# The one-pass matmul helper with its columns in backward order

## The chip, the cores and the metric

The kernel runs on one NeuronCore of a Trainium2 chip. Its time is the device time of one execution in microseconds (us). The kernel before has a median of 864.19 us over three runs (864.02 to 864.34).

## The reference

Two stacked blocks act on 256 rows of width 1024, everything in fp32, batch 1, depth 1 and depth 2.

```python
def first_block(...):                       # 16 meta rows go ahead of x: 272 rows
    z = rms_norm(h_res) @ w_in              # 4 branch inputs, their gates, 4 x 1024 mixing gates
    m = sum(sigmoid(gl[b] + gate_bias[b]) * (branch_b(z) @ w_out_b) for b in pool, mla, conf, short conv)
    return (h_res + rms_norm(m @ w_o))[:, 16:]

def second_block(...):                      # layer 0: gated linear attention, layer 1: MoBA attention
    for i in range(2):
        y = gla_mixer(x) if i == 0 else moba_mixer(x)
        x = layer_norm(ALPHA * x + y)
        x = layer_norm(ALPHA * x + (silu(x @ w_gate) * (x @ w_up)) @ w_down)     # hidden width 2816
```

The work is mostly dense products with weights that are read once: `w_in`, the branch outputs, `w_o`, the attention projections, and two feed-forward layers.

## The kernel before, in words

Products must keep nearly fp32 accuracy, and the kernel gets it out of TensorE's one-pass format (fp32r). Each operand is held as two such parts: a high part, the value rounded by ScalarE (line 1272 for weights), and a low part, value minus high part, which VectorE computes (line 1709 for weights). A product is then three one-pass matmuls into the same PSUM columns: high x high, high x low, low x high. The helper `exact` (lines 595 to 599) issues these three. "Stationary" is the side that is loaded into the array as weights of a matmul, "moving" the side that streams through it column by column; PSUM columns are written in the order in which the moving columns come.

Weights come as 512 KB slots of 128 x 1024 values into a ring of nine (`staged`, with the parts `w_hi` and `w_lo`). SyncE's queue loads the slots in a fixed order; a slot is free for the next load when TensorE's semaphore `weights_used` says so. ScalarE and VectorE make the parts some slots ahead (`lead`). TensorE's program is one list written out by hand, stage after stage, and waits for semaphores only.

`exact` is called in these places:
- `t_slot` (lines 601 to 613): weights stationary, turned activations moving, 256 columns (x rows), 272 (with the meta rows) or 258 (the short convolution's rows, which begin two columns ahead of the 256, at column 14 of a 272-column row). It serves the input products and gates of the first block, and parts of the later ones.
- `y_slot` and `y_mla` (lines 885 and 982): the branch outputs, 256 columns.
- `n_slots` and `n_product` (lines 725 and 743): activations stationary, weights moving, 512 columns, for products whose result is wanted row by row.
- `down_half` (line 1133): the second feed-forward product, 512 columns; the very last quarter of the last layer is cut into two of 256, one of which goes to the bank `misc`.

Not through `exact` go: the first z product (`first_slots`, line 657), the wide stage of the feed-forward (`wide_slot`, lines 624 to 647, in which one matmul of 512 columns has the x high parts in its first 256 columns and the low parts in the others, followed or preceded by one of 256), the row-major first products (`n_first`, lines 688 to 723), the transposes, and the small products in full fp32.

`acc` is PSUM for the products, two pairs of two banks; a pair is written for one output while the other is read by ScalarE or VectorE. `misc` is four banks for everything small. A reader waits for the semaphore of the last matmul that writes its banks. The operands of `exact` are two-dimensional slices (partitions, columns) whose columns lie in one run.

Of the kernel before, what the change touches and what calls it, by code (L numbers as in the profile page):

```python
# [187 lines left out]
def lead_of(at):  # L188

    return min(LEAD, 3 + at // 2)  # L190


def hybrid_stack(nc, d, out):
    with ExitStack() as ctx:
# [389 lines left out]
        def _(pe):  # L584
# [9 lines left out]

            def exact(dst, st_hi, st_lo, mv_hi, mv_lo, start, stop):

                pe.matmul(dst, st_hi, mv_hi, start=start, stop=False)  # L597
                pe.matmul(dst, st_hi, mv_lo, start=False, stop=False)  # L598
                return pe.matmul(dst, st_lo, mv_hi, start=False, stop=stop)  # L599

            def t_slot(sl, p, half, mv_hi, mv_lo, kcs=4, last=True, halves=2, first=True):

                ready(sl)
                n = mv_hi.shape[-1]
                hi = w_hi[:, sl.ring(), :].rearrange("p (c n) -> p c n", c=4)
                lo = w_lo[:, sl.ring(), :].rearrange("p (c n) -> p c n", c=4)
                for b in range(halves):
                    for c in range(kcs):
                        cols = slice(b * P, b * P + P)
                        mm = exact(acc[:, p, b, 0:n], hi[:, c, cols], lo[:, c, cols],  # L610
                                   mv_hi[:, half * 4 + c, :], mv_lo[:, half * 4 + c, :],
                                   start=first and c == 0, stop=last and c == kcs - 1)
                mm.then_inc(weights_used, 1)
# [111 lines left out]
            def n_slots(stage, names, st_hi, st_lo, lo=0, hi=None):  # L725

                for i in range(lo, COUNT[stage] if hi is None else hi):
                    sl = Slot(FIRST[stage] + i, i)
                    q, name = i % 4, names[i // 4]
                    if q == 0:  # L730
                        open_out(name)
                    ready(sl)
                    for c in range(2):
                        cols = slice(c * 512, c * 512 + 512)
                        for t in range(TILES):
                            rows = slice(t * P, t * P + P)
                            k = q * 2 + c
                            mm = exact(acc[:, pair(name), t, :], st_hi[:, k, rows], st_lo[:, k, rows],
                                         w_hi[:, sl.ring(), cols], w_lo[:, sl.ring(), cols],
                                         start=k == 0, stop=k == KC - 1)  # L740
                    mm.then_inc(weights_used, 1)

            def n_product(stage, tag, st_hi, st_lo, chunks_ready):
# [3 lines left out]
                def quarter(i, t):  # L747

                    q, name = i % 4, names[i // 4]
                    sl = Slot(FIRST[stage] + i, i)  # L750
                    rows = slice(t * P, t * P + P)
                    if t == 0:
                        ready(sl)
                    for c in range(2):
                        cols = slice(c * 512, c * 512 + 512)
                        k = q * 2 + c
                        mm = exact(acc[:, pair(name), t, :], st_hi[:, k, rows], st_lo[:, k, rows],
                                   w_hi[:, sl.ring(), cols], w_lo[:, sl.ring(), cols], start=k == 0, stop=k == KC - 1)
                    if t == 1:
                        mm.then_inc(weights_used, 1)  # L760
                    elif q == 3:
                        mm.then_inc(s["tail_part"], 1)
# [311 lines left out]
            for j in range(4):  # L1074
                b = open_bank("o%d" % j)
                t = j // 2
                for i in range(2):
                    hd = j % 2 * 2 + i
                    dst = b[:, i * DV:(i + 1) * DV]
# [173 lines left out]
        def _(act):  # L1253
# [21 lines left out]
            def lead(sl):  # L1275
                round_slots(sl.at + lead_of(sl.at) + 1)
# [410 lines left out]
        def _(dve):  # L1687
# [24 lines left out]
            def lead(sl):  # L1712
                split_slots(sl.at + lead_of(sl.at) + 1)
# [877 lines left out]
```

## Time and profile before

| | |
|---|---|
| median of three runs | 864.19 us |
| the profiled execution's own time | 864.27 us |
| its span, first to last instruction | 862.5 us |
| PE (TensorE matmuls) busy | 850.2 us, 99% |
| PEld (weight loads, beside PE) busy | 757.6 us, 88% |
| DVE (VectorE) busy | 629.8 us, 73% |
| ACT (ScalarE) busy | 426.5 us, 49% |
| read from HBM | 151.48 MB, 177 GB/s over the span |

One execution is recorded by the profiler. Times within it are microseconds from the span's start. Matmuls are pipelined: the next one starts before the one before has ended, and a record's duration (281 ns for 256 columns) is longer than the step from one start to the next. That step is called the pitch below. PEclk is the TensorE clock that was granted, in tenths of full speed.

### The profile page before, as it was taken

The numbers are of one execution on the slowest core, as the hardware profiler recorded it, in microseconds if no ns is written. First come the engines' busy times: TensorE is split into PE (matmuls) and PEld (weight loads), VectorE is DVE, ScalarE is ACT, GpSimd is POOL, SyncE is SP. The second block draws the span as 40 slices with busy tenths as digits, with TensorE's granted clock in tenths as the row PEclk, the third lists the DMA queues.
The fourth block names the chain that finished last, engine by engine and source line by source line (L and its number), as shares of the span: only waits on it lengthen the run. The fifth ranks groups of instructions, "written<-read, shape, count | busy, mean of one in ns | idle before, by whom it ended". The sixth has DMA issues, their size and how long they took to land.

```text
span 862.5 us, 13049 instructions
## 1 busy us (share of the span) xinstructions
PE 850.2 (99%) x5390; PEld 757.6 (88%) x5390; DVE 629.8 (73%) x880; ACT 426.5 (49%) x613; POOL 79.3 (9%) x81
## 2 busy tenths in 40 slices
PE   8999999999999999999999999999999999999996
PEld 7998999999988987878888988889988888889885
DVE  5999857688586675796777764678987777777445
ACT  6646454456664874435444453256553544445320
POOL 0340100122003001011000000031100200000000
PEclk9999999999999999999999999999999999999998
DMA  9963776664356752557556555386544765665531
GB/s 289 270 188 92 203 203 174 181 184 123 100 169 192 238 171 86 171 169 245 184 184 193 195 186 192 117 278 195 178 142 129 244 189 183 191 195 184 187 118 50
DMA packets 121989, 154.46 MB, mean 179 GB/s; under 512 B 11663, under 2 KB 98090, under 8 KB 121930
## 3 DMA queue, kind: packets, MB, share of 16 engines
q1 hardware_dynamic: 119978, 148.23, 56.4%
q0 software_dynamic: 1872, 5.26, 1.8%
q8 instruction: 43, 0.70, 0.3%
q10 hardware_dynamic: 80, 0.13, 0.0%
q14 instruction: 16, 0.13, 0.0%
HBM read 151.48 MB, written 1.05 MB: 177 GB/s over the span
## 4 chain that ended last, share of the span: by engine, by line
PE 94%; DVE 4%; DMA 1%; issue 0%; ACT 0%; SPq 0%; DVEq 0%
PE acc L597 19%; PE acc L599 19%; PE acc L598 19%; PE acc L635 15%; PE acc L639 8%; PE acc L720 1%; PE acc L717 1%; PE acc L718 1%; PE acc L668 1%; PE misc L798 1%; DMA x<-in_x 1%; DVE x L2191 1%; PE misc L857 1%; DVE y L2172 1%; DMA staged<-in_moba_w_in 1%
## 5 line engine op out<-in xcount | busy, mean ns | idle before, releaser
L1709 DVE TENSOR_TENSOR w_lo<-staged,w_hi 128x1024 fp32r<-128x1024 f32 (+1 forms) x274 | 331.6, 1232 | 134.6 <-ACT w_hi L1272 134.0
L1272 ACT CAST w_hi<-staged 128x1024 fp32r<-128x1024 f32 (+1 forms) x274 | 278.0, 1044 | 90.5 <-DMA staged<-in_ffn_w_down 44.2
L597 PE MATMUL acc<-x_parts,w_hi 128*128 128x256 f32 (+2 forms) x712 | 203.4, 286 | 0.0
L598 PE MATMUL acc<-x_parts,w_hi 128*128 128x256 f32 (+2 forms) x712 | 200.6, 282 | 0.0
L599 PE MATMUL acc<-x_parts,w_lo 128*128 128x256 f32 (+2 forms) x712 | 200.5, 282 | 0.0
L635 PE MATMUL acc<-x_parts,w_hi 128*128 128x512 f32 x576 | 196.3, 393 | 0.0
L639 PE MATMUL acc<-x_parts,w_lo 128*128 128x256 f32 x576 | 149.1, 279 | 0.0
L597 PEld LDWEIGHTS acc<-x_parts,w_hi 128*128 128x128 f32 x712 | 134.4, 189 | 1.7 <-issue 1.0
L598 PEld LDWEIGHTS acc<-x_parts,w_hi 128*128 128x128 f32 x712 | 134.0, 188 | 0.7 <-issue 0.2
L599 PEld LDWEIGHTS acc<-x_parts,w_lo 128*128 128x128 f32 x712 | 134.5, 189 | 0.0
L635 PEld LDWEIGHTS acc<-x_parts,w_hi 128*128 128x128 f32 x576 | 103.3, 188 | 18.4 <-DVE gate_sum L2352 0.2
L639 PEld LDWEIGHTS acc<-x_parts,w_lo 128*128 128x128 f32 x576 | 108.3, 188 | 6.4
L597 PE MATMUL acc<-w_hi,h_hi 128*128 128x512 f32 (+1 forms) x176 | 66.3, 377 | 0.0
L598 PE MATMUL acc<-w_lo,h_hi 128*128 128x512 f32 (+1 forms) x176 | 66.3, 377 | 0.0
L599 PE MATMUL acc<-w_hi,h_lo 128*128 128x512 f32 (+1 forms) x176 | 66.1, 376 | 0.0
L1619 ACT CAST h_hi<-hidden 128x512 fp32r<-128x512 f32 x22 | 13.7, 621 | 70.5 <-DVE hidden L2378 65.0
L597 PEld LDWEIGHTS acc<-w_hi,h_hi 128*128 128x128 f32 x176 | 33.1, 188 | 6.1
L599 PEld LDWEIGHTS acc<-w_hi,h_lo 128*128 128x128 f32 x176 | 33.1, 188 | 6.2
L598 PEld LDWEIGHTS acc<-w_lo,h_hi 128*128 128x128 f32 x176 | 33.1, 188 | 5.9
L2516 POOL TENSOR_TENSOR x_parts<-y,x_parts 128x512 fp32r<-128x512 f32 x8 | 10.4, 1295 | 297.1 <-ACT y L1482 297.1
L1478 ACT CAST x_parts<-misc 128x512 fp32r<-128x512 f32 (+1 forms) x20 | 9.6, 503 | 46.4 <-PE misc L798 46.4
L1609 ACT ACTIVATE h_gate<-gate_sum 128x512 f32<-128x512 f32 x16 | 10.1, 632 | 41.8 <-DVE gate_sum L2352 41.8
(394 smaller groups left out, 1256.0 us busy)
## 6 DMA issues: line engine op xcount, KB each, us to landing
staged<-in_ffn_w_gu SPq DMA_DIRECT2D x88, 512.0 KB, 3.6
staged<-in_w_in SPq DMA_DIRECT2D x58, 512.0 KB, 3.8
staged<-in_ffn_w_down SPq DMA_DIRECT2D x44, 512.0 KB, 3.3
staged<-in_gla_w_in SPq DMA_DIRECT2D x24, 512.0 KB, 4.3
staged<-in_moba_w_in SPq DMA_DIRECT2D x24, 512.0 KB, 3.9
staged<-in_w_o SPq DMA_DIRECT2D x8, 512.0 KB, 3.9
staged<-in_gla_w_out SPq DMA_DIRECT2D x8, 512.0 KB, 3.8
staged<-in_moba_w_out SPq DMA_DIRECT2D x8, 512.0 KB, 3.8
```

The lines of the kernel that those rows point to most:

```text
L597: pe.matmul(dst, st_hi, mv_hi, start=start, stop=False)
L598: pe.matmul(dst, st_hi, mv_lo, start=False, stop=False)
L599: return pe.matmul(dst, st_lo, mv_hi, start=False, stop=stop)
L635: return pe.matmul(acc[:, p, b, :].rearrange("p (s n) -> p s n", s=2), hi[:, c, cols], x_parts[:, :, k, 0:ROWS], start=k == 0, stop=k == K ...
L639: return pe.matmul(acc[:, p, b, 0:ROWS], lo[:, c, cols], x_hi[:, k, 0:ROWS], start=False, stop=False)
L668: mm = pe.matmul(acc[:, pair("z0"), b, 0:KEYS], st[:, c, b * P:b * P + P], mv[:, k, :], start=k == 0 and st is hi and mv is x_hi, stop=k = ...
L1272: nc.scalar.copy(hi, raw).then_inc(rounded, 1)
L1478: nc.scalar.copy(x_hi[:, lo:lo + n, t * P:t * P + P], bank(name)[:, 0:n * P] .rearrange("p (c r) -> p c r", c=n)).then_inc(s["x_rounded"], 1)
L1609: nc.scalar.activation(h_gate[:], gate_sum[:], ACT.Silu).then_inc(s["h_gated"], 1)
L1619: nc.scalar.copy(halves(h_hi, b), hidden[:]).then_inc(s["h_rounded"], 1)
L1709: nc.vector.tensor_tensor(lo, raw, hi, ALU.subtract).then_inc(split, 1)
L2516: nc.gpsimd.tensor_tensor(x_lo[:, 4 * j:4 * j + 4, 0:P], y[:, 0, j * 512:j * 512 + 512] .rearrange("p (c r) -> p c r", c=4), x_hi[:, 4 * j ...
```

## The change

A new function, `backwards`, takes an access pattern and returns the same columns from the last to the first: it starts at the last column and has the step negated. `exact` passes the PSUM destination and the moving sides through it. The stationary sides stay as they were.

```diff
+def backwards(ap):
+    step, n = ap.ap[-1]
+    return bass.AP(ap.tensor, ap.offset + step * (n - 1), list(ap.ap[:-1]) + [[-step, n]])
...
             def exact(dst, st_hi, st_lo, mv_hi, mv_lo, start, stop):
 
+                dst, mv_hi, mv_lo = backwards(dst), backwards(mv_hi), backwards(mv_lo)
                 pe.matmul(dst, st_hi, mv_hi, start=start, stop=False)
                 pe.matmul(dst, st_hi, mv_lo, start=False, stop=False)
                 return pe.matmul(dst, st_lo, mv_hi, start=False, stop=stop)
```

Since both are turned, each product column still lands in the PSUM column that it had.

## Rows read from the trace of the kernel before

**Rows 1.** The page: PE's busy time, granted clock by slice, chain that ended last.

```profile
PE 850.2 (99%) x5390; PEld 757.6 (88%) x5390; DVE 629.8 (73%) x880; ACT 426.5 (49%) x613; POOL 79.3 (9%) x81
...
PEclk9999999999999999999999999999999999999998
...
PE 94%; DVE 4%; DMA 1%; issue 0%; ACT 0%; SPq 0%; DVEq 0%
PE acc L597 19%; PE acc L599 19%; PE acc L598 19%; PE acc L635 15%; PE acc L639 8%; PE acc L720 1%; PE acc L717 1%; PE acc L718 1%; PE acc L668 1%; PE misc L798 1%; DMA x<-in_x 1%; DVE x L2191 1%; PE misc L857 1%; DVE y L2172 1%; DMA staged
...
by line: PE acc L597 19.1%; PE acc L599 19.0%; PE acc L598 19.0%; PE acc L635 15.5%; PE acc L639 7.8%; PE acc L720 1.4%; PE acc L717 1.1%; PE acc L718 1.1%; PE acc L668 0.7%; PE misc L798 0.7%; DMA x<-in_x 0.7%; DVE x L2191 0.6%; PE misc L8
```

**Rows 2.** Waits of PE on other engines: us in total, times, longest.

```profile
PE misc L808 <- POOL w_gk L2450: 1.4, 1, 1.4
PE misc L798 <- DVE x L2191: 1.3, 3, 0.4
PE misc L790 <- DVE rs L1760: 0.6, 1, 0.6
```

**Rows 3.** The chain's end: start, us, what.

```profile
853.81 0.13 PE misc L599
853.97 0.43 DVE y L2218
...
858.63 0.75 DVE x L2191
```

**Rows 4.** Timeline of PE, 256 columns: start, us, instruction.

```profile
100.34 0.28 PE L599 MATMUL acc<-x_parts,w_lo 128*128 128x256 f32 x1
...
142.58 0.28 PE L599 MATMUL acc<-x_parts,w_lo 128*128 128x256 f32 x1
```

**Rows 5.** Timeline of PE, 512 columns, feed-forward of layer 0.

```profile
501.50 0.40 PE L597 MATMUL acc<-w_hi,h_hi 128*128 128x512 f32 x1
...
547.75 0.39 PE L597 MATMUL acc<-w_hi,h_hi 128*128 128x512 f32 x1
```

**Rows 6.** Groups by form on PE, count, busy us, mean ns; and L597 over the span.

```profile
L597 PE MATMUL acc<-x_parts,w_hi 128*128 128x256 f32 x632 | 180.2, 285 | 0.0
L597 PE MATMUL acc<-w_hi,h_hi 128*128 128x512 f32 x154 | 60.2, 391 | 0.0
L597 PE MATMUL acc<-w_hi,x_parts 128*128 128x512 f32 x64 | 26.2, 409 | 0.0
L597 PE MATMUL acc<-x_parts,w_hi 128*128 128x272 f32 x48 | 14.1, 293 | 0.0
L597 PE MATMUL acc<-w_hi,mo_hi 128*128 128x512 f32 x32 | 13.0, 405 | 0.0
L597 PE MATMUL acc<-u_mla_hi,w_hi 128*128 128x256 f32 x32 | 9.2, 287 | 0.0
L597 PE MATMUL acc<-x_parts,w_hi 128*128 128x258 f32 x32 | 9.1, 283 | 0.0
L597 PE MATMUL misc<-w_hi,h_hi 128*128 128x256 f32 x22 | 6.2, 283 | 0.0
L597 PE MATMUL acc<-w_hi,h_hi 128*128 128x256 f32 x22 | 6.1, 279 | 0.0
L597 PE MATMUL acc<-u_sc_hi,w_hi 128*128 128x256 f32 x16 | 4.7, 293 | 0.0
...
0.00:862.50 862.50, 363.41 (x1150) 216.91 (x1150) 1.00 0.59 179
```

**Rows 7.** Timeline of PE, 258 columns that begin at column 14.

```profile
46.87 0.28 PE L597 MATMUL acc<-x_parts,w_hi 128*128 128x258 f32 x1
...
58.23 0.28 PE L599 MATMUL acc<-x_parts,w_lo 128*128 128x258 f32 x1
```

**Rows 8.** Timeline of PE, end of the wide stage.

```profile
486.75 0.39 PE L635 MATMUL acc<-x_parts,w_hi 128*128 128x512 f32 x1
486.98 0.28 PE L639 MATMUL acc<-x_parts,w_lo 128*128 128x256 f32 x1
...
489.88 0.40 PE L635 MATMUL acc<-x_parts,w_hi 128*128 128x512 f32 x1
```

**Rows 9.** Groups by form on VectorE.

```profile
L1709 DVE TENSOR_TENSOR w_lo<-staged,w_hi 128x1024 fp32r<-128x1024 f32 x272 | 330.2, 1236 | 134.6 <-ACT w_hi L1272 134.0
L2352 DVE TENSOR_REDUCE up_sum<-acc 128x512 f32<-128x1024 f32 x20 | 24.4, 1218 | 0.0
```

**Rows 10.** Waits of VectorE and ScalarE: us in total, times, longest.

```profile
DVE w_lo L1709 <- ACT w_hi L1272: 134.0, 115, 3.2
...
ACT w_hi L1272 <- DMA staged<-in_ffn_w_down: 44.2, 26, 2.3
```

## The prediction

> **What bounds the kernel now.** I read the page first, then who waits on TensorE, then its instructions by form, then the starts of single matmuls. The page shows PE busy for 99% of the span, and the chain that ended last lies on PE for 94%; the three lines of the edited helper alone carry 19.1%, 19.0% and 19.0% of that chain, which is 57.1% of 862.5 us or some 492 us [rows 1]. The granted clock is full (2.4 GHz) in every slice but the last [rows 1]. PE waits for another engine only in its first microseconds, 1.4 us at the longest, and before transposes of freshly normalised rows [rows 2]. After PE's last matmul at 853.8 us there follow some 8.7 us of VectorE and store [rows 3]. So from the first weights to 853.8 us the time is the sum of the pitches of PE's matmuls, from one start to the next, and whatever changes a pitch changes the span by the same amount: there is no cover for a longer one.
>
> The pitch, and not the duration of one, is what to price, since a matmul's duration overlaps the next one. I take it from long stretches without a wait. Between the two starts at 100.34 and 142.58 us there are 357 matmuls of 256 columns: 42.24 us / 357 = 118.3 ns [rows 4]. Between 501.50 and 547.75 us there are 204 of 512 columns: 46.25 / 204 = 226.7 ns [rows 5]. At 2.4 GHz, 256 columns are 106.7 ns and 512 are 213.3 ns, so streaming a column per cycle fills the pitch but for 11.7 ns and 13.3 ns.
>
> **The change part by part.** How many instructions it touches: the first of the three matmuls is issued 1150 times [rows 6], so 3450 of the 5390 matmuls [rows 1] are turned round. By form, the first line has 632 + 22 + 22 matmuls of 256 columns with x or hidden parts, 32 + 3 x 16 of 256 with branch rows, 48 of 272, 32 of 258, and 154 + 64 + 3 x 32 of 512 (the two other groups with 32 look as the one shown) [rows 6]. That is 836 calls of about 256 columns and 314 of 512: 2508 and 942 matmuls, and (756 x 256 + 48 x 272 + 32 x 258 + 314 x 512) x 3 = 1.127 million columns. By pitch these are 2508 x 118.3 + 942 x 226.7 ns = 510 us. No instruction, wait, semaphore or DMA is added, removed or moved.
>
> (a) Reading the moving side from the last column down. The same 256 or 512 addresses are read, in one run, with step -1 for +1. No row of this trace has a backward read on PE, so the cost is bounded by neighbours. The kindest: 258-column matmuls, whose x parts start 14 columns into a 272-column row and so at an odd place, have starts at 46.87 and 58.23 us with 95 pitches between them, 119.6 ns each [rows 7], against 118.3 + 2 x 0.42 = 119.1 ns for a well-placed run of 258: where a run starts costs 0.5 ns at most. The next: the wide matmul's 512 columns are two runs of 256 with a jump of one whole set of parts between them. Nine pairs of it and a 256-column one take 489.88 - 486.75 = 3.13 us, 347.8 ns a pair, against 226.7 + 118.3 = 345.0: one break in the order costs 2.8 ns or less [rows 8].
>
> (b) Writing PSUM backward. Again the same addresses, each pair of neighbours still written one straight after the other. VectorE gives the only row where neighbours in time are not neighbours in PSUM: its sum of two halves reads 1024 values that alternate between places 256 columns apart in 1218 ns, against 1236 ns for 1024 that lie in a run [rows 9]. That is another engine, slower per value, and reading; it shows only that order as such need not cost.
>
> (c) The dependence between the three matmuls. Each adds to the column that the one before wrote. All three run backward, so a column is still met again one whole pitch (118.3 ns) later, as before. Were only one turned, the column at the turn would be met at once; that isn't done here. Bank groups that are not written by the helper (the wide stage, the first stage, the row-major first products) hold no helper matmuls, so no accumulation mixes directions.
>
> (d) The consumers. ScalarE and VectorE read a bank after a semaphore on the last matmul of a group, whose last column is now column 0; the event comes with the instruction's end, and that moves only with the pitch. Nothing is issued earlier or later on SP's or POOL's queue.
>
> The value that I take for (a) and (b) together is 0 ns a matmul, because the nearest rows that have the same engine and a full-rate stream, the 258-column ones, differ by half a nanosecond with an odd start and a descending run differs from an ascending one in nothing else that the rows price. The ends of the range of the unknown: below, the whole 11.7 or 13.3 ns that a pitch has beyond its columns could go, 2508 x 11.7 + 942 x 13.3 ns = 41.9 us (to 822 us); nothing in the rows excludes a gain, and nothing says why a direction should touch that gap. Above, a column could take two cycles: 1.127 million x 0.417 ns = 470 us. The sum is the profiled execution's 864.27 us + 0; the median of the three runs, 864.19, lies 0.08 us below, so the forecast is 864.2 us.
>
> A rule that speaks against this: the row of 512-column matmuls shows 226.7 ns for 512 values, so more than two values per nanosecond go to PSUM in each partition [rows 5]. By the Trainium skill (Advanced Engine Details and Errata, section Memory Cachelines) PSUM works in lines of two fp32 values, "Any non-contiguous AP significantly slows down matmuls", and every two consecutive elements should be contiguous. By it the sum is unchanged if a descending pair in one line counts as contiguous, and the result is the first rival if it doesn't. The trace holds no descending write, so it doesn't settle which.
>
> **The rivals.** First, slower: pairs are joined only in ascending order, on the read or on the write side (both run in lockstep, so one is enough). Then every column takes two cycles and the price is the 470 us above: 864.2 + 470 = 1334 us. For it: the full rate of a column per 0.42 ns [rows 4, 5] must come from somewhere wider than one value, and every matmul here writes ascending. Against it: the odd start and the broken run cost almost nothing [rows 7, 8], so whatever joins neighbours isn't tied to a whole aligned run. It decides from any backward column at all, with nothing to absorb it: VectorE and ScalarE would wait, not PE. The page of the Trainium skill cited above (Advanced Engine Details and Errata, section Memory Cachelines) is the one that speaks for it.
>
> Second, slower by little: turning the order costs each matmul a fixed time at its start, as the jump does. At the jump's 2.8 ns, 3450 x 2.8 ns = 9.7 us, 874 us; at half of the gap between matmuls (6 ns), 21 us, 885 us. For it: PE has no slack, so that 0.5 ns a matmul is already 1.7 us. Against it: the jump also leaves one place for another, and a plain descending run has no jump inside; between two matmuls there is one in either direction.
>
> Third, faster: the gap between matmuls is partly the cost of beginning at a run's front, and shrinks. The same 2.8 ns taken off gives 854.6 us. Then the next to be late would be the weights: VectorE's low parts wait 134 us for ScalarE's high parts, and these wait 44 us for the transfers of the down weights [rows 10]. Nothing but the unexplained gap speaks for it.
>
> Fourth, no effect because the pattern is written forward again when it is encoded: turning both sides together is the same product, so that nothing would tell it from the first case in time; 864.2 us.
>
> **How the numbers follow.** A measurement of this kernel can tell about 0.2%, 1.7 us, from no change: 0.5 ns a matmul. No change by streaming at the same pitch 0.62, and by the encoding 0.02: 0.64 within 0.2%. Two cycles a column 0.14, a fixed cost 0.15: slower 0.29. Faster 0.07. The range from 858 to 885 us holds the first and fourth cases, nearly all of the second rival and half of the third; it leaves out the two-cycle case and the edges, some 0.19. The likeliest case's own range is 863 to 865.5 us. The two-cycle time is no part of the range, since its chance is below what may be left out.
>
> **What would show it.** Right: the same two pitches, 118.3 and 226.7 ns, in the same stretches, equal counts on every engine, and the wide stage at 347.8 ns a pair in both. If 512-column pitches come to some 440 ns and PE's share of the chain rises while the wide stage stays, it is the first rival; if both pitches grow by the same few nanoseconds, the second; if by an amount in proportion to the columns, a partial form of the first. A difference in the wide stage or in the row-major first products would be no effect of direction, and would prove my reading of the pitch as PE's own wrong.

## The result: 0.64% slower

The changed kernel takes 869.62 us (median of four runs, 869.35 to 870.96) against 864.11 us before (863.80 to 864.34): ratio 1.0065, 95% interval 1.005 to 1.008. That is 5.5 us, some three times what a measurement of this kernel can tell from no change. It lies in the range (858 to 885 us), but the forecast of no change, to which I gave 0.64, is wrong: the time went the other way, to "slower", which had 0.29.

The page of the changed kernel, by engine, by chain and by group:

```profile
span 867.6 us, 13049 instructions
PE 855.6 (99%) x5390; PEld 758.1 (87%) x5390; DVE 630.4 (73%) x880; ACT 426.8 (49%) x613; POOL 79.7 (9%) x81
...
PE 93%; DVE 4%; DMA 2%; ACT 1%; issue 0%; SPq 0%; DVEq 0%
...
by line: PE acc L603 19.8%; PE acc L604 19.6%; PE acc L605 19.6%; PE acc L641 13.7%; PE acc L645 6.9%; PE acc L726 1.4%; PE acc L723 1.1%; PE acc L724 1.1%; DMA staged<-in_ffn_w_gu 0.9%; PE misc L804 0.7%; PE acc L674 0.7%; DVE w_lo L1715 0
```

Every engine has the instructions that it had, and PE is 5.4 us longer busy (850.2 before [rows 1]). The helper's lines 597 to 599 are 603 to 605 here. Their share of the chain grew and that of the wide stage (L641, L645, which are L635 and L639 before) fell, but a chain's shares also shift when it takes another way through a stretch, here through a weight transfer; they don't say where 5 us went. The pitches do. PE's waits are as short as before, in the view of waits:

```profile
PE misc L814 <- POOL w_gk L2456: 1.4, 1, 1.4
PE misc L804 <- DVE x L2197: 1.2, 3, 0.4
```

The same stretches as in [rows 4], [rows 5], [rows 7] and [rows 8], in the timeline of PE after the change (start, us, instruction). First the 256 columns of the gates, with one branch's output product among them:

```profile
99.81 0.28 PE L605 MATMUL acc<-x_parts,w_lo 128*128 128x256 f32 x1
...
142.09 0.28 PE L605 MATMUL acc<-x_parts,w_lo 128*128 128x256 f32 x1
```

42.28 us / 357 = 118.4 ns, against 118.3. The 512 columns of the first feed-forward's down product:

```profile
503.39 0.40 PE L603 MATMUL acc<-w_hi,h_hi 128*128 128x512 f32 x1
...
551.00 0.40 PE L603 MATMUL acc<-w_hi,h_hi 128*128 128x512 f32 x1
```

47.61 us / 204 = 233.4 ns, against 226.7: here is the loss, 6.7 ns a matmul. The 258 columns:

```profile
46.09 0.28 PE L603 MATMUL acc<-x_parts,w_hi 128*128 128x258 f32 x1
...
57.65 0.28 PE L605 MATMUL acc<-x_parts,w_lo 128*128 128x258 f32 x1
```

11.56 us / 95 = 121.7 ns, against 119.6, 2.1 ns more; there are only 96 of them. The 240 matmuls of 256 columns with branch rows rose by 1.1 to 1.4 ns, by the mean of their steps. And the wide stage, which the change doesn't touch, nine pairs:

```profile
488.67 0.39 PE L641 MATMUL acc<-x_parts,w_hi 128*128 128x512 f32 x1
488.90 0.28 PE L645 MATMUL acc<-x_parts,w_lo 128*128 128x256 f32 x1
...
491.80 0.40 PE L641 MATMUL acc<-x_parts,w_hi 128*128 128x512 f32 x1
```

3.13 us, 347.8 ns a pair, to the digit what [rows 8] gave. The row-major first products, the other ones that are not turned, are as long as before too: in the third of their four stretches the first start and the last but one lie 12.26 us apart before (562.17 and 574.43 us) and 12.28 now (565.79 and 578.07).

The stretches in the down product are the largest block of wide calls; over all wide calls the rise in pitch is smaller, about 5 ns. By the starts of all of them, without steps of 300 ns and more, the forward pitch was 226.8 ns with `m`, `o` or the first layer's `h` as stationary side, 228.0 with `mo`, 228.8 with the second layer's `h`, and 230.9 with x parts. After the change all six groups lie at 233.3 to 233.5 ns: what a backward read has in common is not a price but a level. Weighed by their counts the rises make 4.9 us.

The chain's end is the same 8.7 us of VectorE and store as in [rows 3], 5.1 us later:

```profile
858.88 0.13 PE misc L605
859.04 0.43 DVE y L2224
...
863.70 0.75 DVE x L2197
```

### The profile page after: what moved, and what is told of

Read it like the earlier page. It is cut to its first block, busy times and chain, and to the rows that moved or that the text cites. A ratio compares the mean times of both kernels' runs of the same rounds, so it can differ in the third digit from the quotient of the medians.

```text
span 867.6 us, 13049 instructions
## 1 busy us (share of the span) xinstructions
PE 855.6 (99%) x5390; PEld 758.1 (87%) x5390; DVE 630.4 (73%) x880; ACT 426.8 (49%) x613; POOL 79.7 (9%) x81
## 4 chain that ended last, share of the span: by engine, by line
PE 93%; DVE 4%; DMA 2%; ACT 1%; issue 0%; SPq 0%; DVEq 0%
PE acc L603 20%; PE acc L604 20%; PE acc L605 20%; PE acc L641 14%; PE acc L645 7%; PE acc L726 1%; PE acc L723 1%; PE acc L724 1%; DMA staged<-in_ffn_w_gu 1%; PE misc L804 1%; PE acc L674 1%; DVE w_lo L1715 1%; DMA staged<-in_w_in 1%; PE misc L863 1%; PE misc L1088 0%; ACT w_hi L1278 0%
## 5 line engine op out<-in xcount | busy, mean ns | idle before, releaser
L641 PE MATMUL acc<-x_parts,w_hi 128*128 128x512 f32 x576 | 196.5, 393 | 0.1
L645 PE MATMUL acc<-x_parts,w_lo 128*128 128x256 f32 x576 | 149.1, 279 | 0.0
L641 PEld LDWEIGHTS acc<-x_parts,w_hi 128*128 128x128 f32 x576 | 103.4, 188 | 18.8 <-DVE gate_sum L2358 0.4
L645 PEld LDWEIGHTS acc<-x_parts,w_lo 128*128 128x128 f32 x576 | 108.3, 188 | 6.3
```

Source lines behind the costliest of these rows:

```text
L641: return pe.matmul(acc[:, p, b, :].rearrange("p (s n) -> p s n", s=2), hi[:, c, cols], x_parts[:, :, k, 0:ROWS], start=k == 0, stop=k == K ...
L645: return pe.matmul(acc[:, p, b, 0:ROWS], lo[:, c, cols], x_hi[:, k, 0:ROWS], start=False, stop=False)
```

## The experiments

Two theories stood after the traces: W, that only long runs pay, and F, that each turned matmul pays the same small amount. Beside them, which side pays: the read of the moving side or the write to PSUM.

**Which calls.** The helper turns its operands only for 512 columns, or only for fewer:

```diff
-                dst, mv_hi, mv_lo = backwards(dst), backwards(mv_hi), backwards(mv_lo)
+                if dst.shape[-1] == 512:        # e1_wide_only;  < 512 in e2_narrow_only
+                    dst, mv_hi, mv_lo = backwards(dst), backwards(mv_hi), backwards(mv_lo)
```

> Only the calls with 512 columns run backward; those with 256 to 272 run forward as before. Theory W (the price is one of long runs: 226.7 ns became 233.3 ns in the feed-forward stretch while 256 columns stayed at 118.3): 942 matmuls by 5 to 6.6 ns, so 4.7 to 6.2 us over the kernel before, about 869.3 us. Rival F (a fixed cost of every turned matmul, 5.5 us / 3450 = 1.6 ns): 942 x 1.6 ns = 1.5 us, 865.6 us.

> The complement: only the calls with 256, 258 and 272 columns run backward. Theory W: within 0.6 us of the kernel before, about 864.3 us, with 118.3 ns for the 256 columns of the gate stretch and 226.7 ns for the 512 of the feed-forward. Rival F: 2508 x 1.6 ns = 4.0 us, 868.1 us.

Measured: wide only 868.57 us against 863.80 of the kernel before on the same chip (ratio 1.0056, 1.0041 to 1.0071), narrow only 864.02 us (1.0003, 0.9994 to 1.0013). F falls, and in time W holds; the moved ring, below, shows that length alone is not the reason. The wide calls carry 4.8 us, 5.1 ns for each of 942 matmuls, and the rises in their pitches gave 4.9 us; the 2508 narrow ones 0.2 us, less than can be told from nothing. The feed-forward stretch (start, us, instruction) with the wide calls alone backward, which is 47.60 us / 204 = 233.3 ns:

```profile
502.39 0.40 PE L604 MATMUL acc<-w_hi,h_hi 128*128 128x512 f32 x1
...
549.99 0.40 PE L604 MATMUL acc<-w_hi,h_hi 128*128 128x512 f32 x1
```

With the narrow calls alone backward it has its old pitch:

```profile
501.48 0.39 PE L604 MATMUL acc<-w_hi,h_hi 128*128 128x512 f32 x1
...
547.72 0.39 PE L604 MATMUL acc<-w_hi,h_hi 128*128 128x512 f32 x1
```

46.24 us / 204 = 226.7 ns.

**Which side.** Only the read, or only the write, in all calls:

```diff
-                dst, mv_hi, mv_lo = backwards(dst), backwards(mv_hi), backwards(mv_lo)
+                mv_hi, mv_lo = backwards(mv_hi), backwards(mv_lo)      # e3_read_only
+                dst = backwards(dst)                                   # e4_write_only, instead
```

> All calls of the helper read the moving side backward but write PSUM forward, so that a product's columns land mirrored. Theory R (the read of SBUF in descending order is what costs): 869.6 us and 233.3 ns for 512 columns, as with both turned. Rival P (the descending write to PSUM costs): 864.1 us and 226.7 ns. If only the two together cost, 864.1 us here and in the run with the write alone.

> All calls of the helper read the moving side forward but write PSUM backward (columns land mirrored). Theory R: 864.1 us and 226.7 ns for 512 columns. Rival P: 869.6 us and 233.3 ns. Two costs that add up would show as two parts of 5.5 us in this run and the one with the read alone.

Measured: read only 869.11 us (1.0064, 1.0049 to 1.0079), write only 863.96 us (1.0001, 0.9992 to 1.001). The same stretch, with the read alone turned:

```profile
503.01 0.40 PE L603 MATMUL acc<-w_hi,h_hi 128*128 128x512 f32 x1
...
550.61 0.40 PE L603 MATMUL acc<-w_hi,h_hi 128*128 128x512 f32 x1
```

and with the write alone turned:

```profile
501.29 0.40 PE L603 MATMUL acc<-w_hi,h_hi 128*128 128x512 f32 x1
...
547.54 0.39 PE L603 MATMUL acc<-w_hi,h_hi 128*128 128x512 f32 x1
```

47.60 us / 204 = 233.3 ns for the read, 46.25 / 204 = 226.7 ns for the write. R holds in both runs: the price is that of the descending read of SBUF, and the descending write to PSUM cost nothing that can be told from noise.

**Does the read collide with the weight load?** A weight load runs beside each matmul and reads SBUF as well. In the inner chunks of the wide calls the stationary side is cut to 32 columns, which shortens the load from 188 to 108 ns:

```diff
+                if dst.shape[-1] == 512 and not (start or stop):
+                    dst, st_hi, st_lo = dst[0:32], st_hi[:, 0:32], st_lo[:, 0:32]
```

> As the changed kernel, but in the products with 512 columns all matmuls of the inner chunks (not the first and last of a sum) use only the first 32 of the 128 stationary columns, so 96 of 128 result rows lack those chunks. The weight load beside the running matmul is shorter, the moving read is the same. Theory C (the descending read collides with the weight load's own read of SBUF, which runs beside it): the difference from the forward twin of this run shrinks from 6.6 ns a matmul to some quarter of it, about 1.7 ns, in the feed-forward stretch. Rival L (the descending read itself is slower, whoever else reads): the difference stays 6.6 ns.

> The forward twin: the kernel before with the same 32 of 128 stationary columns in the inner chunks of the 512-column products (96 of 128 result rows lack those chunks). Theory C: below 226.7 ns a matmul, by as much as the forward read collides too; 220 to 225 ns. Rival L: 226.7 ns unchanged if the gap of 13.3 ns beyond streaming has nothing to do with the load.

Measured: 868.82 us backward, 866.03 us forward, one run each, 863.59 for the kernel before beside them. Backward and forward, in that order:

```profile
502.92 0.40 PE L605 MATMUL acc<-w_hi,h_hi 128*128 128x512 f32 x1
...
550.52 0.40 PE L605 MATMUL acc<-w_hi,h_hi 128*32 128x512 f32 x1
```

```profile
501.27 0.40 PE L604 MATMUL acc<-w_hi,h_hi 128*128 128x512 f32 x1
...
548.48 0.39 PE L604 MATMUL acc<-w_hi,h_hi 128*32 128x512 f32 x1
```

Backward it is 47.60 / 204 = 233.3 ns as with all 128 columns; forward it is 47.21 / 204 = 231.4 ns. The difference shrank to 1.9 ns, which is the number that C gave, but not for its reason: the backward read gained nothing from the shorter load, and the forward read lost 4.7 ns with it. Neither theory expected that. C as put is not borne out, and L, which wanted both unchanged, is right only of the backward half. With 32 columns the matmul also fills a quarter of its result rows; these runs don't separate that from the shorter load.

**Does the place matter?** The constants are placed ahead of the weight ring, not behind it, in the changed kernel and in the one before:

```diff
+        const = place("const", CONST_N)
+        cursor[0] += 64
         ring_at = cursor[0]
...
-        const = place("const", CONST_N)
```

> As the changed kernel, with the constants placed ahead of the weight ring, so that the ring begins 7040 bytes later and each 2 KB moving run begins at a multiple of 1 KB instead of 128 bytes past one; all else moves by 64 bytes. If what costs is the crossing of a boundary of 1 KB by a descending run (rival L in its address form), the runs cross one fewer and 233.3 ns falls to some 230 ns. Theory C: the place of the two reads against each other changes, the pitch of backward runs can change either way by a few ns; if it stays 233.3 ns to the tenth, neither place matters.

> The forward twin of the moved ring: the kernel before with the same placement. Rival L in its address form: 226.7 ns changes by less than 1 ns and the time is 864 us. Theory C: the forward pitch, which was 226.7 ns with hidden parts and 230.9 ns with x parts as stationary side, changes with the place too; the two may trade.

Measured: 868.25 us backward and 864.19 us forward, one run each beside 863.59. The forward run's stretch:

```profile
500.45 0.40 PE L598 MATMUL acc<-w_hi,h_hi 128*128 128x512 f32 x1
...
548.05 0.40 PE L598 MATMUL acc<-w_hi,h_hi 128*128 128x512 f32 x1
```

47.60 / 204 = 233.3 ns, read forward. Backward it is 233.3 ns too (from 502.40 to 550.00 us), as at the old place. So 226.7 ns belongs to reading forward at the old place, not to reading forward as such. Theory C had the forward pitch change with the place, and it did; rival L had it within 1 ns of the old one. (All else moves by 64 bytes, so which operand's place counts is not shown.) The moved forward kernel is not 6 us slower for all that, since the other wide groups lost less (0.1 to 2.2 ns) and the last matmuls of 256 columns, with weights as moving side, sped up from 120.0 to 113.5 ns. The boundary of 1 KB, which I had named for L, explains nothing: the descending runs crossed fewer and paid the same.

Those last matmuls tell more. In all other calls of the helper 256 columns are activations and 512 are weights, so that the length of the run and the kind of the moving side change together; only here do 256 columns of weights move. In the kernel before, in the changed one, with the ring moved and read forward, and with it moved and read backward, in that order:

```profile
850.89 0.28 PE L597 MATMUL misc<-w_hi,h_hi 128*128 128x256 f32 x1
...
853.65 0.28 PE L599 MATMUL misc<-w_hi,h_lo 128*128 128x256 f32 x1
```

```profile
856.00 0.28 PE L603 MATMUL misc<-w_hi,h_hi 128*128 128x256 f32 x1
...
858.72 0.28 PE L605 MATMUL misc<-w_hi,h_lo 128*128 128x256 f32 x1
```

```profile
851.01 0.28 PE L598 MATMUL misc<-w_hi,h_hi 128*128 128x256 f32 x1
...
853.62 0.28 PE L600 MATMUL misc<-w_hi,h_lo 128*128 128x256 f32 x1
```

```profile
854.89 0.28 PE L604 MATMUL misc<-w_hi,h_hi 128*128 128x256 f32 x1
...
857.65 0.28 PE L606 MATMUL misc<-w_hi,h_lo 128*128 128x256 f32 x1
```

Over 23 steps these are 120.0, 118.3, 113.5 and 120.0 ns. (Those of 256 columns in `acc` go the same way: 117.9, 119.2, 113.7 and 119.1 ns by the mean of their steps.) At the old place the backward read cost the ones shown nothing; at the new one it costs them 6.5 ns, as much as 512 columns pay at the old place, while the 512 of the first feed-forward's stretch pay nothing there. So "only long runs pay" is true of this kernel's placement and is no rule. What fits both lengths is that a forward read can lie below the level of a backward one where the place lets it, and that turning it loses just that. This is argued from the pitches; what makes a place good is not shown.

**Which order inside the run.** The wide calls read their 512 columns in groups, with the order of the groups and the order inside a group turned separately; PSUM is written forward:

```diff
+def in_groups(ap, size, groups_back, inside_back):
+    step, n = ap.ap[-1]
+    count = n // size
+    first = (size * (count - 1) if groups_back else 0) + (size - 1 if inside_back else 0)
+    dims = [[-step * size if groups_back else step * size, count], [-step if inside_back else step, size]]
+    return bass.AP(ap.tensor, ap.offset + step * first, list(ap.ap[:-1]) + dims)
...
+                if dst.shape[-1] == 512:
+                    mv_hi, mv_lo = in_groups(mv_hi, 16, False, True), in_groups(mv_lo, 16, False, True)
+                    dst = in_groups(dst, 16, False, False)
```

(The others have 16, True, False; 256, True, False; and 4, False, True.)

> Only the 512-column calls differ from the kernel before: their moving side is read in 32 groups of 16 columns, the groups in ascending order, the columns inside each group backward (PSUM is written forward, so columns land permuted). Theory G (a descending read costs because far ahead lying groups come in descending order): the feed-forward stretch has a forward pitch, 226.7 to 231.5 ns, and the time is 864 to 866 us. Rival N (each backward step between neighbours costs, some 0.013 ns a column): 233.3 ns, 868.6 us. Should both orders of this pair of runs cost more than 234 ns, the pattern of two dimensions has a price of its own.

> The complement for the 512-column calls: 32 groups of 16 columns in descending order, each read forward inside (PSUM written forward). Theory G: 233.3 ns and 868.6 us, as with a plain backward read. Rival N: 226.7 to 231.5 ns, 864 to 866 us.

> The 512-column calls read their moving side as two halves of 256 columns, the upper half first, each forward (PSUM written forward). If the price grows with the descending run's length, one backward step in 512 leaves a forward pitch plus at most the 2.8 ns of the jump in the wide stage: 226.7 to 232 ns, 864 to 867 us. If it is the matmul's end far from the next one's beginning that costs (a backward matmul ends where a forward one begins), half of the way is saved here and the pitch lies between, some 230 ns.

> As the run with 16-column groups in ascending order and the columns inside read backward, with groups of 4 columns (16 bytes) instead; 512-column calls only, PSUM written forward. The 16-column groups cost 266.7 - 213.3 = 53.3 ns a matmul, 1.67 ns for each of 32 groups, or 1.04 ns a group over the 233.3 ns of a plain backward read. Theory J (a price for every step from the front of one group to the back of the next): 128 groups, 233.3 + 133 = 366 ns to 213.3 + 213 = 427 ns a matmul, the time 990 to 1050 us. Rival U (a unit of 4 columns is fetched whole, and the order inside it is free): 226.7 to 231.5 ns, 864 to 866 us.

Measured, one run each: 901.49 us (16 columns backward inside ascending groups), 868.44 us (descending groups of 16, forward inside), 863.37 us (upper half first), each beside 863.61 us of the kernel before; and 863.34 us (4 columns backward inside ascending groups) beside 864.12 us. The stretch in the four, in this order:

```profile
514.63 0.43 PE L608 MATMUL acc<-w_hi,h_hi 128*128 128x512 f32 x1
...
569.03 0.43 PE L608 MATMUL acc<-w_hi,h_hi 128*128 128x512 f32 x1
```

```profile
502.33 0.40 PE L608 MATMUL acc<-w_hi,h_hi 128*128 128x512 f32 x1
...
549.93 0.40 PE L608 MATMUL acc<-w_hi,h_hi 128*128 128x512 f32 x1
```

```profile
500.71 0.40 PE L608 MATMUL acc<-w_hi,h_hi 128*128 128x512 f32 x1
...
546.97 0.39 PE L608 MATMUL acc<-w_hi,h_hi 128*128 128x512 f32 x1
```

```profile
500.61 0.40 PE L608 MATMUL acc<-w_hi,h_hi 128*128 128x512 f32 x1
...
546.87 0.39 PE L608 MATMUL acc<-w_hi,h_hi 128*128 128x512 f32 x1
```

That is 54.40 / 204 = 266.7 ns, 47.60 / 204 = 233.3 ns, and twice 46.26 / 204 = 226.8 ns. One jump to a lower half costs nothing, so the distance between a matmul's end and the next one's beginning is not it. Columns turned inside groups of 4 (16 bytes) cost nothing: U holds, J falls. Groups of 16 that descend, read forward inside, cost what the plain backward read costs, as G said. But 16 columns turned inside ascending groups cost 40 ns, six times the price, which G had at nothing: G is only half right, and N falls, since 4 columns turned step backward three times in four and are free. What fits all four is this: order within 16 bytes is free, and a run pays for the order in which its pieces of 16 bytes come. A steady descent of them costs 6.7 ns here, and so do three steps up and one of seven down, again and again; three steps down and one of seven up cost 40 ns. What rule joins these prices is not shown.

The Trainium skill (Advanced Engine Details and Errata, section Memory Cachelines) says that SBUF has lines of 16 bytes, that accesses which stay on one line run at full performance, and that at least two hits on a line are needed to absorb the memory's latency. The free order inside 4 columns (226.8 ns) agrees with the size of the line. The groups of 16 are not covered by the rest: every line there gets four hits in a row, and yet a matmul takes 266.7 ns. Here the measurement decides: the order of the lines has a price as well.

## Why the prediction was right in its range and wrong in its case

**What bounds the kernel** was right: PE's pitches make the time and nothing covers a longer one. The rises in the pitches of the wide groups add up to 4.9 us, and 4.8 us is what the run with the wide calls alone lost.

**(a) The moving read, taken at 0 ns,** is the step that failed. I took the 258-column row as the nearest, as it has a full-rate stream and an odd start. It could say nothing of the wide calls, and here nearly the whole price is theirs: 0.1 ns for the 256 columns of the gates, 6.7 ns for 512 in the largest stretch. My sum had 942 wide matmuls in a term of their own with a pitch of their own, and gave both terms one price. It also took the 226.7 ns of [rows 5] for what 512 columns cost on this engine, with a gap of 13.3 ns that I called unexplained and let stand. The other wide groups had up to 230.9 ns forward, the moved ring shows the same forward stretch at 233.3 ns, and the shorter weight load at 231.4 ns: 226.7 was a value that this placement gives, and the change lost it. The backward read lay at 233.3 ns at both places and with both loads that were tried. That the loss was small and not a second cycle for each column was right. That 869.62 us lies in the range is partly luck: its upper end stood for a fixed cost of every matmul, and that is not what happened.

**(b) The write** at 0 ns was right: 863.96 us against 863.80 with the write alone. **(c) and (d)**, the dependence and the readers, were right in so far as nothing else moved: equal counts, waits as short as before, 347.8 ns in the wide stage, the row-major first products as long as before.

**The rivals.** The first (two cycles a column, 1334 us) is refuted on both sides, read and write. The Trainium skill's rule on PSUM (Advanced Engine Details and Errata, section Memory Cachelines), which spoke for it, does not bite on a descending run: with the write alone turned, 512 columns kept 226.7 ns. The second (a fixed cost of each matmul, 874 us at 2.8 ns) is nearest in time and wrong in kind, as the narrow calls, nearly three quarters of those turned, added 0.2 us. The third and the fourth are refuted by the time and by the pitch. None of them had a price that some calls pay in full and others not at all; of the signs that I gave, "in proportion to the columns" was closest, and that is not it either. My forecast had the sign that would refute it, two equal pitches, and it was the wide one that refuted it.

**Still open:** why the same matmuls pay for the descent at one place and not at another, and what sets the gap between two matmuls at all (6.8 to 20.0 ns beyond the columns without the groups of 16 turned inside, by place, by the weight load's size and by order). That the read of SBUF and its order by 16 bytes are at stake is shown; that two reads collide was only argued, and the shorter weight load spoke against the simple form of it. Turning the stationary side was not tried.

## What to carry to other kernels

Price a change of access order by form, not per instruction: take the pitch of each shape from a long stretch without waits, and give each shape, with each place of its operands, its own unknown. A pitch of one-pass matmuls has some nanoseconds that belong to where the operands lie and not to the work, so a re-placement or a turned order can lose or win 3% of a stage with no instruction changed; compare pitches before and after, not busy time. When a pattern must run against the grain, turn it inside 16 bytes or by large blocks, both of which were free for 512 columns here, and not in between.

## What the hardware showed that I had not expected

- 512 columns read forward took 226.7, 231.4 or 233.3 ns a matmul in the first feed-forward's down product, by place and by the size of the weight load beside them, at the same granted clock (mean 0.996 or 0.997 in each of these runs).
- Read backward, they took 233.3 ns there in all of four settings: both sides turned, the read alone, a quarter of the stationary columns, the moved ring.
- Blocks of 16 columns turned inside, in ascending order: 266.7 ns. Blocks of 4 turned inside: 226.8 ns.
- 256 columns with weights as moving side went from 120.0 to 113.5 ns when the ring moved, and back to 120.0 when they were also read backward.
- No version beat the kernel before: the two lowest, at 863.34 and 863.37 us, ran once each and lie within its own spread (863.29 to 864.70).
